# Exponentials of one attention tile in two sets of four heads, with seven score buffers

## The reference, cut to what matters

```
out attention:  p = softmax([s_band, s_meta, sink]);  out = p @ v      (8 heads of 64)
out experts:    act = gelu(u_sel . h) * softmax(scores)
                out = sum over 8 x 16 chosen experts of act * v_sel
```

## Time and profile before

| what | value |
|---|---|
| median of the runs shown | 1171.18 us |
| span of the profiled execution | 1174.8 us |
| instructions | 14173 |
| PE / VectorE / ScalarE / POOL busy | 955.4 / 733.2 / 535.4 / 297.2 us |
| table loads, lines L1555 and L1464 | 58 and 51, 1283 ns each |
| gathers of expert rows | 256; their queue q0 took 56.8% of the DMA engines' span |

### The profile page before, as it was taken

One profiled execution on the slowest core, in us unless ns is written; L12 is line 12 of the kernel. 1 busy time (PEld: TensorE's weight loads), 2 busy tenths in 40 slices (PEclk: granted clock), 3 DMA queues, 4 the chain that ended last, 5 costly groups with the idle time before them and its releaser, 6 DMA issues.

```text
span 1174.8 us, 14173 instructions
## 1 busy us (share of the span) xinstructions
PE 955.4 (81%) x4746; PEld 422.0 (36%) x4746; DVE 733.2 (62%) x2006; ACT 535.4 (46%) x1409; POOL 297.2 (25%) x298
## 2 busy tenths in 40 slices
PE   4998987866767578775798977898877799999998
PEld 4765532212222222221133332223333234554564
DVE  5876665689998575557745656656667742342353
ACT  5332259733424534434564654464674732322231
POOL 0000222353444343333332223333223610000000
PEclk9898997787877888887798988999897799999998
DMA  8044898899999999999999997999998987637630
GB/s 316 12 177 153 351 391 306 324 399 388 407 380 370 426 421 425 423 422 421 415 418 425 426 424 295 424 423 419 425 424 334 421 318 299 223 144 298 233 144 19
DMA packets 51881, 395.36 MB, mean 337 GB/s; under 512 B 5808, under 2 KB 10544, under 8 KB 11616
## 3 DMA queue, kind: packets, MB, share of 16 engines
q0 software_dynamic: 37536, 270.91, 56.8%
q1 hardware_dynamic: 13696, 122.83, 26.1%
q10 hardware_dynamic: 576, 0.72, 0.2%
HBM read 393.38 MB, written 1.05 MB: 336 GB/s over the span
## 4 chain that ended last, share of the span: by engine, by line
PE 47%; DVE 20%; DMA 16%; ACT 12%; issue 4%; POOL 1%; SPq 0%; DVEq 0%; ACTq 0%
PE bank L1825 16%; DMA expert_rows<-in_peer_uv,peer_idx 15%; PE bank L1486 9%; DVE expert_rows L1426 7%; PE bank L1155 4%; ACT L1555 3%; PE bank L2098 2%; ACT L1464 2%; PE bank L2057 2%; DMA x_res<-in_x 2%; PE bank L708 1%; DVE r L970 1%; PE bank L1696 1%; PE bank L1732 1%; PE bank L412 1%
## 5 line engine op out<-in xcount | busy, mean ns | idle before, releaser
L1486 PE MATMUL bank<-expert_rows,peer_diag 64*64 64x512 f32 x2048 | 328.5, 731 | 132.1 <-ACT peer_diag L1471 126.3
L1501 POOL DMA_INDIRECT expert_rows<-in_peer_uv,peer_idx x256 | 284.0, 1109 | 553.7 <-PE bank L1486 504.2
L1426 DVE CUSTOM_DVE_ANT_0 expert_rows<-expert_rows,HN 128x1024 f32<-128x1024 f32 x256 | 309.4, 1221 | 103.9 <-DMA expert_rows<-in_peer_uv,peer_idx 100.9
L1825 PE MATMUL bank<-w_ring,b_xt 128*128 128x512 f32 (+1 forms) x576 | 278.4, 610 | 3.4 <-DVE b_xt L1626 3.4
L1464 ACT ACTIVATE peer_dots<-peer_dots 128x1 f32<-128x1 f32 x256 | 51.5, 201 | 329.9 <-DVE peer_dots L1426 328.7
L1486 PEld LDWEIGHTS bank<-expert_rows,peer_diag 64*64 64x64 f32 x2048 | 63.2, 150 | 311.1 <-ACT peer_diag L1471 235.3
L1825 PEld LDWEIGHTS bank<-w_ring,b_xt 128*128 128x128 f32 x576 | 101.7, 195 | 137.9 <-issue 131.2
L1471 ACT ACTIVATE peer_diag<-peer_eyes,peer_dots 128x64 f32<-128x64 f32 x256 | 89.0, 348 | 8.8 <-PE bank L1486 0.5
L1555 ACT ACT_TABLE_LOAD x58 | 74.4, 1283 | 20.9 <-DMA cols<-in_cols 5.5
L1465 ACT ACTIVATE peer_dots<-peer_dots,peer_ex 128x1 f32<-128x1 f32 x256 | 75.4, 295 | 8.3
L1464 ACT ACT_TABLE_LOAD x51 | 65.4, 1283 | 1.9 <-DVE peer_dots L1426 0.9
(11 more groups left out here) (408 smaller groups left out, 1159.2 us busy)
## 6 DMA issues: line engine op xcount, KB each, us to landing
w_ring<-in_w_in_e SPq DMA_DIRECT2D x16, 2048.0 KB
w_ring<-in_w_in_o SPq DMA_DIRECT2D x14, 2048.0 KB
w_ring<-in_w_query SPq DMA_DIRECT2D x8, 2048.0 KB
w_ring<-in_w_out SPq DMA_DIRECT2D x4, 2048.0 KB
w_ring<-in_w_out_e SPq DMA_DIRECT2D x4, 2048.0 KB
w_ring<-in_w_out_o SPq DMA_DIRECT2D x4, 2048.0 KB
w_ring<-in_w_in SPq DMA_DIRECT2D x2, 2048.0 KB
expert_rows<-in_peer_uv,peer_idx POOLq DMA_INDIRECT x256, 16.7
```

What stands on the lines that cost most here:

```text
L1426: t.dve.tensor_tensor_reduce(u, u, t.HN[:, it // PH, :], 1.0, 0.0, ALU.mult, ALU.add, self.dots[:, it, k:k + 1]).then_inc(*self.dotted.add())
L1486: ins = t.pe.matmul(t.PS[2 * T + r][HALF * c:HALF * (c + 1), :], self.diag[tokens, d % self.RD, :], self.slot(n)[tokens, D + c * 512:D + ( ...
L1501: t.pool.indirect_dma_start(self.slot(n), None, t.dram["peer_uv"], bass.IndirectOffsetOnAxis(ap=self.idx[:, it, k:k + 1], axis=0)).then_in ...
L1825: ins = t.pe.matmul(pa[:, 0:n], L.xt[:, k, :], t.w.at(i, k, 0, n), start=k == 0, stop=k == KT - 1)
```

## The change

Tile 0's attention stays as it was. For tile 1 the exponentials of heads 0 to 3 come together at step 5, those of heads 4 to 7 at step 9, with the exponential of the sinks behind them in that step (before: step 10). Turning starts at step 6 (before: 3), placing at 7 (4), mixing at 8 (5); the stage has 17 steps in place of 14. Seven score buffers in place of three hold the heads meanwhile. The meta columns are copied at steps 6 (heads 0 to 3 in one copy) and 10 (heads 4 to 6, then head 7) in place of one by one. The subtraction for the sinks follows the last minimum in its step. The seven buffers are laid over two more tiles (`mT` and `zs`) that the closing of each tile's mixer uses.

```diff
-    R = 3
+    R = (3, 7)[T]
...
-    sums, exps, turns, places, mixes = ((0, 1, 2, 3, 4), (1, 2, 3, 4, 5))[T]
+    sums, turns, places, mixes = ((0, 2, 3, 4), (1, 6, 7, 8))[T]
+    groups = {n + 1: (n,) for n in range(NU)} if T == 0 else {5: (0, 1, 2, 3), 9: (4, 5, 6, 7)}
+    runs = {n + 2: ((n, n + 1),) for n in range(NU)} if T == 0 else {6: ((0, 4),), 10: ((4, 7), (7, 8))}
...
-            n = i - exps - 1
-            if 0 <= n < NU:
-                t.dve.wait_ge(*expd.at(n + 1))
+            for n, end in runs.get(i, ()):
+                t.dve.wait_ge(*expd.at(end))
...
+                    ins = t.dve.tensor_copy(t.pm[T][:, h:h + end - n, :],
+                                            t.as_[T][:, n % R:n % R + end - n, 0:width][:, :, meta])
...
-            if n == NU:
+            if n == (NU, NU - 1)[T]:
                 t.dve.wait_ge(*least.at(NU))
...
-            if exps <= i < NU + exps:
-                n = i - exps
+            for n in groups.get(i, ()):
                 t.act.wait_ge(*least.at(n + 1))
                 logs(t)
...
-            if i == NU + exps:
+            if i == (NU + 1, 9)[T]:
                 t.act.wait_ge(*sunk.at(1))
...
-    as1, pm1 = over.sb("as1", [P, 3, SEQ + META]), over.sb("pm1", [P, PH, META])
-    t.mT, t.zs = (area.sb(x, [P, 4, P]) for x in ("mT", "zs"))
+    as1, pm1 = over.sb("as1", [P, 7, SEQ + META]), over.sb("pm1", [P, PH, META])
```

More of the change, by code:

```diff
@@ L625, in dve @@
         for i in range(NU + mixes + 1):
-            n = i - exps - 1
-            if 0 <= n < NU:
-                t.dve.wait_ge(*expd.at(n + 1))
+            for n, end in runs.get(i, ()):
+                t.dve.wait_ge(*expd.at(end))
                 h = sets[n][0]
-                ins = t.dve.tensor_copy(t.pm[T][:, h:h + 2 * E - 1:2, :],
-                                        t.as_[T][:, n % R, 0:E * width].rearrange("p (e w) -> p e w", e=E)[:, :, meta])
-                ins.then_inc(*least.add()) if n == NU - 1 else t.dch.mark(ins)
+                if T == 0:
+                    ins = t.dve.tensor_copy(t.pm[T][:, h:h + 2 * E - 1:2, :],
+                                            t.as_[T][:, n % R, 0:E * width].rearrange("p (e w) -> p e w", e=E)[:, :, meta])
+                else:
+                    ins = t.dve.tensor_copy(t.pm[T][:, h:h + end - n, :],
+                                            t.as_[T][:, n % R:n % R + end - n, 0:width][:, :, meta])
+                ins.then_inc(*least.add()) if end == NU else t.dch.mark(ins)
             n = i - sums
@@ L2634, in both_blocks @@
     t.zT, t.sg = (area.sb(x, [P, 4, P]) for x in ("zT", "sg"))
+    t.mT, t.zs = (area.sb(x, [P, 4, P]) for x in ("mT", "zs"))
     over = Room(t.nc, start, area.at)
-    as1, pm1 = over.sb("as1", [P, 3, SEQ + META]), over.sb("pm1", [P, PH, META])
-    t.mT, t.zs = (area.sb(x, [P, 4, P]) for x in ("mT", "zs"))
+    as1, pm1 = over.sb("as1", [P, 7, SEQ + META]), over.sb("pm1", [P, PH, META])
     t.small, t.gb = area.sb("small", [P, 15, ST]), area.sb("gb", [P, 4])
```

## The result

The changed kernel took 1160.5 us (median of 7 runs, 1156.03 to 1164.75) where the kernel before took 1171.18 us (7 runs, 1168.73 to 1176.59). The ratio is 0.9899, 95% interval 0.9876 to 0.9923: about 1% faster, 10.7 us by the medians and 11.8 us by the ratio. The forecast was 1161 us, with a range of 1156 to 1170.

The account below looks back on a forecast made before the run. ScalarE's table loads were taken to bound tile 1's attention, then VectorE the scan, then DMA. An earlier write (2.5 us) plus three rows done (7.5 us) gave 10.0 us off the 1171.2 median: 1161 us, range 1156 to 1170.

Parts of the forecast that it names:

- Fourteen loads off ScalarE, 18.1 us: Tile 1's attention: 9 visits with 18 table loads become 2 with 4, 18.1 us less on ScalarE.
- The sets: Tile 1's attention: first set of exponentials takes 3.7 us until 185.9, second with sinks 3.9 us until 199.8.
- the signs: What would show the forecast right, among them two VectorE waits of 2 to 4 us for exponentials in tile 1's attention.
- The write: Tile 1's attention output written after row 23 at 215.7 us, 2.5 us earlier; PE decides; ends of range 213.5 and 222.9.
- The high clock: Late in tile 1's attention, PE taken mostly at its high level: a step costs 2.2 us, against 3.7 at the low.
- The drain: Skill page's 1.38 us of draining per table load: 37 us would go by it; the forecast used the trace instead.
- Three rows at 2.49 us: Behind the scan, where DMA bounds: three more expert rows already done save 3 x 2.49 = 7.5 us.
- The scan ends 2.5 us earlier: Tile 1's state-space scan takes as long as before and ends 2.5 us earlier, with 3 more rows gathered.
- The bound by DMA, 14.5 us: Tile 1's attention window left 14.5 us of DMA unused; that is the most the change can give.
- What is late next: Tile 1's query scores come after rows 101 to 127: at most a short wait at row 102; last copy around 514 to 517.
- The stages behind: Behind the attention: scan still at 95% VectorE, then row starts of 2.49 us, each released by its gather.
- Rival D: Gain there at row 84 but lost later, in 560 to 880 us with PE and DMA nearly full; 1171, chance 0.10.

Follow-up runs that it names:

- twenty needless loads: Changed kernel plus 20 needless table loads, at expert rows 87 to 105 (1160.9 us, 0.9912) or, in another run, 41 to 59 (1163.4 us, 0.9916).
- the early sets: Against the kernel before: tile 1's exponentials in four sets of two heads at steps 2, 4, 6, 8, everything behind on its old row; 1161.5 us, 0.9919.
- four sets of two: Against the changed kernel: tile 1's exponentials in four sets of two heads at steps 3, 5, 7, 9, turns from step 4; 1159.8 us, 0.9891.
- the two that put the queries back: Changed kernel with tile 1's queries on their old rows: two closing steps per row (1164.3 us, 0.9932) or 1.18 scan steps per row (1163.4 us, 0.9918).
- the idle rows: Kernel before with three (1169.9 us, 0.9987) or four (1169.4 us, 0.9979) expert rows inserted behind tile 1's attention, nothing else emitted in them.
- two closing steps: Changed kernel with two steps of the closing of tile 1's mixer per row in place of one; 1164.3 us, 0.9932.
- PE kept busy: Changed kernel with 11 needless matmuls on PE at the head of each of steps 6 and 10 of tile 1's attention; 1161.9 us, 0.9906.
- the loads put back: Changed kernel with 14 needless table loads, two in each of seven steps of tile 1's attention, same order otherwise; 1168.1 us, 0.9972.

## Why the prediction was right, point by point

- **Fourteen loads off ScalarE, 18.1 us.** Right: the two lines have 109 loads before and 95 after; ScalarE lost 18.4 us.
- **The sets.** The first ended at 185.84 (forecast 185.9), the second at 199.5 with its sinks (199.8). VectorE's first wait was 1.69 us and not 3.0, outside the 2 to 4 us of the signs: its dot of row 12 had waited 1.03 us for a gather. Two small errors cancelled: a head costs 0.51 us in a set, not 0.61, and the set began 0.2 us later.
- **The write.** 214.85 (212.88 in the second trace) for 215.7. The second lies outside the 213.5 to 219.7 that the forecast gave as a sign. The number was right in part by luck. The high clock was argued from PE being busy without a pause from 190.8 to 202 us. In the trace PE is busy 5.5 of 8 us from 192 to 200 and pauses 3.40 us ahead of 201.75; the granted clock is 0.50 from 187 to 192 and from 200 to 206 us, 0.93 between and 0.99 from 206 to 215. PE had less of a backlog than forecast, and so could do with less of the high clock. The forecast named PE as the last. In the first trace the write does wait for PE, but only 0.31 us; VectorE was ready at 214.5, after waits of 0.84 and 0.73 us for the gathers of rows 22 and 23. In the second trace it does not wait for PE at all.
- **The drain of the Trainium skill's page "ScalarE: Activation LUTs"** (section "What ACT_TABLE_LOAD costs"), some 1.38 us more for each load, is in no row: after a load the next instruction starts 1.29 us later (182.40 to 183.69). In 385 to 440 us the kernel with twenty needless loads has 16 loads more than the changed kernel (22 to 6). At the page's 2.66 us each they would take an estimated 43 us; ScalarE is busy 20.2 us more, and there two loads in a row and the instruction behind them start 1.29 us apart (399.08, 400.37, 401.66).
- **The rule of the Trainium skill's page "TensorE: Matmul & The Clock Gate"** (section "HAM oscillation"), that pauses of PE put the next burst on the low clock, is borne out by the trace: 3.40 us of pause and then 1.98 us for the row. A pause of 1.76 us ahead of the mixing was followed by 1.98 us too. There it costs time: the first group of the mixing took 2.2 us more than before in the first trace and 0.7 in the second, and VectorE waited for it.
- **Three rows at 2.49 us.** The sum by this account (time of the write, plus 2.49 us for each row more) gives 3.4 + 7.5 = 10.9 us for the changed kernel and 9.7 + 0 = 9.7 us for the early sets; measured are 11.8 and 9.5. It holds less well elsewhere: 8.3 us for four sets of two (measured 12.8, 10 to 16), 11.1 and 12.0 for the two that put the queries back (8.0 and 9.6), -0.6 and -1.6 for the idle rows (1.5 and 2.5), all outside the interval, if some barely.
- **The scan ends 2.5 us earlier.** The write's gain was taken over to the scan as it was. The scan took as long as before, 136.4 us, but it ended 0.3 us earlier in the first trace and 4.2 in the second, and 1.7 to 2.6 us earlier in four others with the same attention (two closing steps, PE kept busy, and the two with twenty loads). The mean of the six is 2.2, so 2.5 is about right, and a single trace can't tell it from 0 or 4. In the first trace 1.4 us were lost ahead of the mixing, where VectorE waited 3.7 us for the gathers of rows 24 to 26 (before 0.3), and 2.4 in its first group. With the end of the scan in place of the write (and 2.49 us for each row more by then) the sum is 7.8 and 11.6 us for the two traces of the changed kernel, 4.2 for the loads put back, 9.7 for four sets of two, 10.6 for the early ones, 1.4 and 0.5 for three and four idle rows. All but the first lie within the interval of the time saved.
- **The bound by DMA, 14.5 us.** Nothing came above 12.8 (10 to 16), so nothing speaks against it. No kernel tested it from above.
- **What is late next.** Here the forecast was loose. It said at most a short wait; it was 1.6 us, and DMA lost some 3 us of its lead there in the first trace and 1.4 in the second. In the end this did not show. The last scores were kept at 527.5 and 521.2, not 514 to 517: row 127 started at 529.9 before, so even with the full 10 us they could not be earlier than 520. That was a slip of arithmetic, without weight in the sum.
- **The stages behind.** Right: VectorE is busy 95.5% of the scan, and DMA is full from 380 us on but for the wait at row 102 (416 GB/s from 380 to 560 us). Rival D (the gain lost later) fell: row 255's dot came 8.7 us earlier in the first trace and 13.0 in the second.

What stays open: why moving the queries back by three rows brings nothing or loses up to 3 us; how much of the 3.3 us of the order comes from the rows gained by the end of the scan (the idle rows' 1.4 and 0.5 us would fit); and what the changed kernel would gain if the first group of its mixing ran at the high clock. All are about as large as the intervals.

## What to carry to other kernels

Here an instruction was worth time only in the stage where its engine was the bound: read the busy share in a window of that stage, not over the span. Ask next what the stages behind are bound by: here DMA, so the most that can be won is the DMA time that the stage had left idle (14.5 us). With DMA busy 0.96 to 0.98 of the stage, the number of loads mattered no more: four sets of two heads, with twice the loads, did as well as two sets of four. When work is moved to later steps, count both the time at which it ends and what else is done by then, and take that time where the next long stage starts, not where the first one ends: between the two the changed kernel lost up to 3 us. And check what a needless instruction costs by itself before its result is read as that of the clock.

## What the runs showed of the hardware

- Exponentials of 128x272 with a sum follow each other every 0.51 us, though instruction and read of the sum take 0.52 and 0.19 us: the read starts 0.09 us before its exponential ends, and its other 0.10 us lie beside the next one.
- Two executions of the same program were 1.7 us of DMA traffic apart at 180 us, and 6 us at row 140; those two took 1164.2 and 1161.4 us, and the medians of the kernel's two measurements lie 0.8 us apart.
- The granted clock of PE was raised from 0.68 to 1.00 over 19 us by 22 needless matmuls (128x272, float32). Each shows as two records and each eleven of them held PE for 5.3 us; the time stayed the same within the interval.
- The same group of eight matmuls (128x512) took 3.70 us at a granted clock of 1.00 and 4.3 to 5.9 us where PE had paused ahead of it and began at the low level.
- Two table loads in a row and the instruction behind them start 1.29 us apart, with nothing between.
